# Swapping the halves of the rotated rows by on-chip transfers instead of by permutation matmuls

## The reference, cut to what matters

```python
def apply_partial_rope(x, cos, sin):
    xr = x[..., :ROT_DIM].astype(jnp.float32)            # ROT_DIM = 32
    x1, x2 = xr[..., : ROT_DIM // 2], xr[..., ROT_DIM // 2:]
    rot = jnp.concatenate([x1 * cos - x2 * sin, x2 * cos + x1 * sin], axis=-1)
    return jnp.concatenate([rot.astype(x.dtype), x[..., ROT_DIM:]], axis=-1)
...
    k, v = jnp.split(rms_norm(x, kv_norm) @ w_kv, 2, axis=-1)
    k = apply_partial_rope(k.reshape(bsz, seq, N_HEADS, HEAD_DIM), cos, sin)
...
    q = apply_partial_rope((h @ w_q).reshape(bsz, seq, N_HEADS, HEAD_DIM), cos, sin)
```

## Time and profile before

| | us |
|---|---|
| median of three runs | 1744.65 (1742.34 to 1746.13) |
| the profiled execution, its own time | 1747.92 |
| its span | 1746.2 |
| PE busy in the span | 1541.4 (88%) |
| DVE busy | 872.5 (50%) |
| ACT busy | 658.7 (38%) |
| key rotation, first PE matmul to last DVE sum | 448.07 to 457.35 |
| query rotation, first PE matmul to last DVE sum | 499.38 to 508.76 |

### The profile page before, as it was taken

One profiled execution on the slowest core, in us unless ns is written; L12 is line 12 of the kernel. 1 busy time (PEld: TensorE's weight loads), 2 busy tenths in 40 slices (PEclk: granted clock), 3 DMA queues, 4 the chain that ended last, 5 costly groups with the idle time before them and its releaser, 6 DMA issues.

```text
span 1746.2 us, 34026 instructions
## 1 busy us (share of the span) xinstructions
PE 1541.4 (88%) x14278; PEld 1321.5 (76%) x14278; DVE 872.5 (50%) x1259; ACT 658.7 (38%) x869; POOL 149.6 (9%) x188
## 2 busy tenths in 40 slices
PE   9999999999999999999999999899998565665558
PEld 8999899988988989997898899688975232332334
DVE  5865456645656546665576689876641010101011
ACT  5545354435445435543456745535441000000001
POOL 5900000000000000000006001130110000000000
PEclk9999999999999999999999999899999777787789
DMA  8765656774743766664455244102899999999995
GB/s 250 254 204 172 192 155 184 216 265 154 252 149 118 269 193 188 187 193 165 134 165 174 73 150 151 40 27 74 303 399 413 430 430 429 430 431 432 430 431 248
DMA packets 238129, 417.09 MB, mean 239 GB/s; under 512 B 13698, under 2 KB 213929, under 8 KB 228009
## 3 DMA queue, kind: packets, MB, share of 16 engines
q1 hardware_dynamic: 237817, 414.59, 66.0%
q10 hardware_dynamic: 176, 0.53, 0.1%
HBM read 414.04 MB, written 1.05 MB: 238 GB/s over the span
## 4 chain that ended last, share of the span: by engine, by line
issue 47%; PE 41%; DVE 4%; POOL 4%; ACT 3%; DMA 1%; DVEq 0%; POOLq 0%; SPq 0%; ACTq 0%
PE bank L429 5%; PE bank L430 4%; PE bank L431 4%; PE bank L445 2%; PE bank L447 2%; PE bank L446 2%; PE bank L1922 2%; PE bank L1075 1%; PE bank L1077 1%; PE bank L1076 1%; PE bank L761 1%; POOL ang L912 1%; POOL ang L913 1%; PE bank L457 1%; PE bank L458 1%
## 5 line engine op out<-in xcount | busy, mean ns | idle before, releaser
L250 DVE TENSOR_TENSOR w_lo<-w_raw,w_hi 128x2048 fp32r<-128x2048 f32 (+2 forms) x178 | 402.9, 2267 | 246.3 <-ACT w_hi L243 246.2
L243 ACT ACTIVATE w_hi<-w_raw 128x2048 fp32r<-128x2048 f32 (+2 forms) x178 | 333.8, 1879 | 155.3 <-DMA w_raw<-in_ffn_w_down_dram 58.9
L429 PE MATMUL bank<-h_hi,w_hi 128*128 128x256 f32 x1168 | 328.0, 281 | 6.6 <-DVE h_lo L639 3.8
L431 PE MATMUL bank<-h_hi,w_lo 128*128 128x256 f32 x1168 | 326.9, 280 | 0.0
L430 PE MATMUL bank<-h_lo,w_hi 128*128 128x256 f32 x1168 | 326.9, 280 | 0.0
L429 PEld LDWEIGHTS bank<-h_hi,w_hi 128*128 128x128 f32 x1168 | 220.8, 189 | 8.1 <-issue 7.8
L431 PEld LDWEIGHTS bank<-h_hi,w_lo 128*128 128x128 f32 x1168 | 221.4, 190 | 0.0
L430 PEld LDWEIGHTS bank<-h_lo,w_hi 128*128 128x128 f32 x1168 | 219.4, 188 | 0.0
L2800 PE MATMUL bank<-w_exp_four,xeT 128*32 128x256 f32 x1600 | 133.6, 503 | 95.0 <-DMA w_exp_four<-in_w_up_dram 57.3
L2800 PEld LDWEIGHTS bank<-w_exp_four,xeT 128*32 128x32 f32 x1600 | 66.0, 143 | 161.7 <-issue 86.0
L2933 ACT ACTIVATE sg<-bank 128x256 f32<-128x256 f32 x16 | 6.1, 383 | 391.5 <-PE bank L2800 391.5
(11 more groups left out here) (536 smaller groups left out, 3101.2 us busy)
## 6 DMA issues: line engine op xcount, KB each, us to landing
w_exp_four<-in_w_up_dram SPq DMA_DIRECT2D x13, 4096.0 KB, 33.5
w_exp_four<-in_w_down_dram SPq DMA_DIRECT2D x13, 4096.0 KB, 33.5
w_exp_four<-in_w_gate_dram SPq DMA_DIRECT2D x12, 4096.0 KB, 33.3
w_raw<-in_ffn_w_gu_dram SPq DMA_DIRECT2D x88, 512.0 KB, 5.0
w_raw<-in_w_in_dram SPq DMA_DIRECT2D x54, 512.0 KB, 4.7
w_mod<-in_w_mod_dram SPq DMA_DIRECT2D x24, 1024.0 KB, 7.4
w_raw<-in_ffn_w_down_dram SPq DMA_DIRECT2D x44, 512.0 KB, 4.2
w_raw<-in_mem_w_kv_dram SPq DMA_DIRECT2D x32, 512.0 KB, 4.5
```

Source lines behind the costliest of these rows:

```text
L243: e.activation(whi[slot][:, 0:w], raw[slot][:, 0:w], ACT.Copy).then_inc(S["hi_ready"], 1)
L250: e.tensor_tensor(wlo[slot][:, 0:w], raw[slot][:, 0:w], whi[slot][:, 0:w].bitcast(F32), ALU.subtract).then_inc(S["lo_ready"], 1)
L429: e.matmul(dst, whi[slot][:, lo:hi_], bh[:, k, :], start=begin, stop=False)
L431: ins = e.matmul(dst, wlo[slot][:, lo:hi_], bh[:, k, :], start=False, stop=end)
```

## The change

The matrix `swap1` and its eight matmuls are gone. The halves change places by DMA: ACT issues two transfers for each half of the heads (four heads, 16 partitions by 4 KB each, 64 KB) from `kT` or `qT` to `xn_rope`, one for features 16 to 31 to partitions 0 to 15, one the other way. The sign stands in the sine table now, which ACT makes with the scale `sign1` (-1 for partitions 0 to 15, 1 for 16 to 31). DVE makes for each half of the heads a product with the sine, one with the cosine, and a sum, six instructions of 32 by 1024 instead of four of 32 by 512 and two of 32 by 2048. Line numbers with 11xx in this section are those of the changed kernel (L1141 the transfers, L1169 the products, L1172 the sum).

```diff
-    swap1 = place("swap1", [ROT, ROT], F32)
+    sign1 = place("sign1", [ROT, 2], F32)
...
+            signed = {"scale": sign1[:, 0:1]} if (j, q) == (0, 1) else {}
+            t_rope = act.do(lambda e, ...: e.activation(
+                tab[:, q, :], angles[0:n_, 2 * j + q, :], ACT.Sin, **signed), t_ang, t_sign)
...
+    def swap_rows(buf, tmp, hf):
+        ks = slice(4 * hf, 4 * hf + 4)
+        def run(e):
+            for to, from_ in ((0, ROT // 2), (ROT // 2, 0)):
+                e.dma_start(tmp[to:to + ROT // 2, ks, :], buf[from_:from_ + ROT // 2, ks, :]).then_inc(rows_swapped[hf], 16)
+        return run
+    def copy_and_swap(buf, tmp, ready):
+        evacs = st.evac_a
+        swap = swap_rows(buf, tmp, 0)
+        def chunk(e, c, u, ch):
+            if c == 2:
+                e.wait_ge(S["act_evac"], evacs + 2)
+                e.wait_ge(*ready)
+                swap(e)
+            return copy_fm(buf)(e, c, u, ch)
+        return chunk
+    def rope_rows(buf, tmp, tab, evacs):
+        swaps["n"] += 1
+        swap = swap_rows(buf, tmp, 1)
+        def last_swap(e):
+            e.wait_ge(*evacs)
+            swap(e)
+        act.raw(last_swap)
+        for hf in range(2):
+            landed = (rows_swapped[hf], 32 * swaps["n"])
+            b3, t3 = (v_[0:ROT, 4 * hf:4 * hf + 4, :] for v_ in (buf, tmp))
+            times = lambda v_, q: dve.do(lambda e: e.tensor_tensor(v_, v_, tab[:, q:q + 1, :].broadcast_to((ROT, 4, SEQ)), ALU.mult),
+                                         landed, t_rope, evacs)
+            ts, tc = times(t3, 1), times(b3, 0)
+            t = dve.do(lambda e, b3=b3, t3=t3: e.tensor_tensor(b3, b3, t3, ALU.add), ts, tc)
+        return t
...
-    gemm(4, cols(A["w_kv"]), ..., act_chunk=copy_fm(kT), ready=[th], act_ready=[th2])
+    gemm(4, cols(A["w_kv"]), ..., act_chunk=copy_and_swap(kT, xn_rope, th2), ready=[th], act_ready=[th2])
-    t1 = rope_fm(kT, KT, rope1, swap1, ROT, [t_k, th2], xn_rope)
+    t1 = rope_rows(kT, xn_rope, rope1, t_k)
-    gemm(4, cols(A["moba_w_q"][0]), ..., act_chunk=copy_fm(qT), ready=[th2], act_ready=[t_memkv],
+    gemm(4, cols(A["moba_w_q"][0]), ..., act_chunk=copy_and_swap(qT, xn_rope, t_memkv), ready=[th2], act_ready=[t_memkv],
-    t1 = rope_fm(qT, KT, rope1, swap1, ROT, [t_q, t_memkv], xn_rope)
+    t1 = rope_rows(qT, xn_rope, rope1, t_q)
```

More of the change, by code:

```diff
@@ L553, in build @@
     pool.do(lambda e: e.memset(ident[:, :], 0.0))
-    t = pool.do(lambda e: e.memset(swap1[:, :], 0.0))
+    t = pool.do(lambda e: e.memset(sign1[:, :], -1.0))
+    t_sign = pool.do(lambda e: e.affine_select(out=sign1[:, :], in_=sign1[:, :], compare_op=ALU.is_ge, fill=1.0,
+                                               base=ROT // 2 - 1, pattern=[[0, 2]], channel_multiplier=-1), t)
     t_id = pool.do(lambda e: e.affine_select(out=ident[:, :], in_=ident[:, :], compare_op=ALU.not_equal,
@@ L564, in half_swap @@
         return t
-    t = half_swap(swap1[:, :], ROT, t_id)
-    t_swap = t
+    t_swap = t_id
     for n_ in range(4):
@@ L972, in build @@
         for q in range(2):
-            t_rope = act.do(lambda e, j=j, q=q, tab=tab, n_=n_: e.activation(tab[:, q, :], angles[0:n_, 2 * j + q, :], ACT.Sin), t_ang)
+            signed = {"scale": sign1[:, 0:1]} if (j, q) == (0, 1) else {}
+            t_rope = act.do(lambda e, j=j, q=q, tab=tab, n_=n_, signed=signed: e.activation(
+                tab[:, q, :], angles[0:n_, 2 * j + q, :], ACT.Sin, **signed), t_ang, t_sign)
     gemm(4, cols(A["conv_w_out"][0]), tm_chunk(a_hi, a_lo), dve_chunk=add_tm(x), ready=[t_conv_out])
@@ L1127, in rope_fm @@
         return dve.do(lambda e: e.tensor_tensor(b3, b3, tmp[0:rows, 0:tiles, :], ALU.add), t)
+    rows_swapped = [nc.alloc_semaphore(f"rows_swapped{hf}") for hf in range(2)]
+    swaps = {"n": 0}
+    def swap_rows(buf, tmp, hf):
[29 more added lines that the diff above has]
+        return t
     mem_attention(0, h2, (h_hi, h_lo), lambda k: kT[:, k, :], 1)
@@ L1138, in build @@
                          behind=tiles_of[th])
-    gemm(4, cols(A["w_kv"]), fm_chunk(h_hi, h_lo), act_chunk=copy_fm(kT), ready=[th], act_ready=[th2])
+    gemm(4, cols(A["w_kv"]), fm_chunk(h_hi, h_lo), act_chunk=copy_and_swap(kT, xn_rope, th2), ready=[th], act_ready=[th2])
     t_k = act_evacs()
@@ L1149, in build @@
     t_memkv = split_features(turn_rows(xn, rows), lambda k: col("norm_memkv", 8 + k), [all_used()])
-    gemm(4, cols(A["moba_w_q"][0]), fm_chunk(*h2), act_chunk=copy_fm(qT), ready=[th2], act_ready=[t_memkv],
+    gemm(4, cols(A["moba_w_q"][0]), fm_chunk(*h2), act_chunk=copy_and_swap(qT, xn_rope, t_memkv), ready=[th2], act_ready=[t_memkv],
          beside={j: mod_load(0, j) for j in range(4)})
```

## The result

The changed kernel takes 1759.51 us (median of 4 runs, 1756.18 to 1762.26), the kernel before 1743.49 (4 runs, 1741.78 to 1746.13). The ratio is 1.0107, with an interval of 1.0079 to 1.0135: **slower by 1.1%, some 16 to 19 us**, where 5 us less had been forecast. The profiled execution took 1761.23 us, with a span of 1759.5; its counterpart before has 1746.2.

A forecast was written before the change was run, and what follows sets the result against it. PE, busy 88% of the span, was taken as the bound; 2.5 us at the keys plus 4.4 at the queries, less 1.5 of clock, gave 5.4 us off the median 1744.65: 1739.3 us, range 1736.2 to 1743.3.

The forecast's parts named there:

- What bounds the kernel: Whole kernel: PE is busy for 88% of the span, no other engine for more than half.
- PE's part of the sum: Permutation and slow matmuls removed on PE: 5.2 us at the keys, 6.9 at the queries, 12.1 if PE alone decided.
- the case with both pauses: Rival: both new PE pauses, at keys and queries, cost lower clock; gain 3.9 us, 1740.8 us; chance 0.37.
- DVE: Rotation on DVE: six instructions of 1.23 us, about 7.2 us together against 7.35 before, so the rotation hardly ends earlier.
- V3: Keys: V3's split stands behind the rotation, so PE waits 2.7 us and 2.5 of 5.2 us are left.
- The softmax and the turning: Queries: PE waits 1.1 us before the scores, 3.0 before turning the probabilities; the softmax starts 4.4 us earlier.
- The transfers: On-chip swaps at keys and queries: 0.46 us of ACT per issue, landing in 3.2 us, delaying nobody.
- spare of 2.2 us: Second half of the heads, keys and queries: its transfers land 2.2 us before DVE is ready for them.
- late landing: Rival: transfers land one to three us late at both places, so the rotation's second half waits; 1742.3 us; chance 0.08.
- weight loads ahead: Rival: transfers stand behind weight loads and take 15.1 us; 12.5 us lost, 1757.2 us; chance 0.03.
- The clock: PE's two new pauses, 2.7 and 3.0 us: one is followed by lower clock, costing 1.5 us.
- the forecast's 5.4: Main case: 6.9 us from both places, less 1.5 us for one pause's lower clock, 1739.3 us; chance 0.42.

The follow-up runs named there:

- experiments 9 and 10: The kernel before (9) and the changed kernel (10), both with the features 64 bytes higher than in the kernel before: 1759.57 us and 1755.51 us.
- experiment 1: The changed kernel with 96 unused bytes behind sign1, so later tensors have their addresses of the kernel before: 1740.69 us, ratio 1.0006.
- Experiment 4: The changed kernel with the 96 bytes put back and V3's split ahead of the memory's normalization: 1736.41 us, ratio 0.9973 to the kernel before.
- experiment 8: The kernel before with 32 bytes ahead of w_raw, moving weights and features together: 1740.40 us, ratio 1.0001.
- experiments 13 and 14: Changed kernel, V3's split first, M3's low part behind the first softmax, features 32 bytes lower (13) or 96 higher (14) than before: 1751.98 and 1742.67 us.
- experiment 12: Changed kernel with the 96 bytes put back, V3's split ahead of the memory's normalization, M3's low part behind the first softmax: 1735.99 us, 0.9967 to the kernel before.
- 7: The changed kernel with the 96 bytes put back behind x, so only x and the rope tables stay moved: 1743.81 us, ratio 1.0020 to the kernel before.
- 6: The changed kernel with the sign columns inside neg_half, features 128 bytes lower than in the kernel before: 1739.92 us, ratio 0.9993 to the kernel before.
- experiment 3: The changed kernel with 32 bytes behind sign1, features 64 bytes lower than in the kernel before: 1751.47 us, ratio 1.0076 to the kernel before.

## Why the prediction was wrong, point by point

- **What bounds the kernel**: right. **PE's part of the sum** (12.1 us): the permutation's 7.8 us went, with the slow stretches behind it. But the slow stretch at the queries, 2.9 us of the sum, is in two of six traces of kernels with the permutation only, and the one at the keys in five. Without the former the two places won 1.7 us in the traces of experiments 9 and 10, where the case with both pauses had 3.9.
- **DVE**: right. 7.24 us for six instructions, forecast 7.2, at 1.21 each (1.23).
- **V3**: the mechanism right. A wait of 3.07 us in the changed kernel, 2.95 in experiment 1, where 2.7 was expected. The profile puts it down to ACT; but the `w_hi` that it names is a later chunk's, and PE started at 472.30, when the low part of V3, the first of these three (2.29 us each), had just ended at 472.2:

```profile
469.91 6.86 DVE L250 TENSOR_TENSOR w_lo<-w_raw,w_hi 128x2048 fp32r<-128x2048 f32 x3 [2.23 <-ACT w_hi L243]
```

  Experiment 4 shows that the order of the queues was at fault.
- **The softmax and the turning**: right. 0.72 and 2.67 us of wait against 1.1 and 3.0; at the scores the profile names ACT's `keys2a`, which ended at 517.91, but DVE's last sum ended at 517.89: the two came together.
- **The transfers**: mis-sized and harmless. The landing is not 3.2 us, and the issue is not 0.46. The tile's rows, issue in ns (min/median/max) and first and last start, with the landing:

```profile
L1141 ACTq DMA_DIRECT2D xn_rope<-kT x4: 514/604/1132, 446.6 to 453.7; - x4
L1141 ACTq DMA_DIRECT2D xn_rope<-qT x4: 514/560/612, 500.0 to 507.0; - x4
DMA to landing us min/median/max: 3.9/4.7/6.1
```

  The spare of 2.2 us over 3.2 covers the median, and DVE shows no idle time before any of its six instructions at the keys. A pair of issues held ACT for up to 1.76 us (446.61, the pair ahead of K2's evacuation) where 0.9 was expected; the split behind was early enough. The late landing and the weight loads ahead (1757.2 us, which by accident is close to the result) did not happen: the slower time has another cause, and the number agreeing would have misled whoever did not look at 418 us.
- **The clock**: the forecast let one pause cost 1.5 us. Both did (the second case, 0.37), in experiment 10 by 1.8 and 1.5 us of its lead. The 4.1 us between the medians of experiments 9 and 10 are near that case's 3.9 and the forecast's 5.4, and too uncertain to choose between them.
- **The step that failed** is a term that the sum (2.5 us at the keys, 4.4 at the queries, less 1.5 of clock) put at nothing without a reason. It counted what the change adds and removes in the queues, and took `sign1` in place of `swap1`, the first lines of the diff, for no cost at all, without naming what lies behind them in memory. This term measured some 18 us (ratio 1.0107 for the change, 1.0006 with the 96 bytes put back; 2.9 ns on 6,500 starts are 19), against 2 to 4 for all the others together, and of the other sign. The range (1736.2 to 1743.3) and the 0.02 for slower had no room for it, as each case in them began at the rotation. A rival "the 96 bytes matter" had no price in any row of before; but the rows that could have warned were there: the pace was two-valued (0.118 for the keys' products, 0.114 behind the queries, both in the prediction's own sums) and I used both without asking why the same instruction has two.

## What to carry to other kernels

Where tensors are placed one behind the other, an edit that resizes a small one moves every later one; keep the addresses (pad, or put the new tensor last) when you test an idea, and time the pad alone as a control. When a change costs or brings more than its place can explain, compare the start of the same instruction in both traces well ahead of the edit, and then the distance of PE's starts, not durations or busy shares. And try a few paddings between stationary and moving operands of a matmul-bound kernel: here two pads alone put the same kernel 19 us apart (ratios 1.0001 in experiment 8, 1.0111 in 9), more than any edit of the order won.

Read a small win against the scatter of single executions, too: a stretch of low clock that stands in one trace (here the 2.9 us behind the query permutation) may be missing in the next.

## What the runs showed of the hardware

- A stream of 128x256 float32 matmuls at full clock starts every 113.3 to 120.0 ns, by the signed distance in SBUF between its two operands (table under experiments 13 and 14). The Trainium skill (TensorE: Matmul & The Clock Gate, "Wait — 56ns, not 53.3ns?") gives N ÷ 2.4 GHz and about 2.5 ns from start to start; for 256 columns that makes an estimate of 109.2 ns. All measured paces here lie above it, and they are not one number.
- At shifts 0 and -128 the pace has two levels, 113.3 and 117.8 ns, and one can hold for long within an execution (201 to 472 us in the kernel before); at +64 there is one, 120.0.
- Waits of PE of 2.4 to 3.9 us were mostly followed by a clock of 0.50, for 3.4 us (2.95 in experiment 1, 2.4 and 2.7 in 10, 3.9 in 7, 2.67 in the change) or 6.8 us (3.07 in the change, 3.6 in 6); one of 2.7 in experiment 1 and two of 2.7 in experiment 3 by none. At 1.6 us none fell in experiment 12; but 1.2 us without matmuls from 970.6 us on were followed there by 3.4 us at 0.50.
- Eight 32x32x512 matmuls, in which PE was shown busy for 3.6 to 4.0 us, were followed by a clock of 0.50 in seven of twelve places (six traces), for 3.4 or 6.8 us.
- An on-chip transfer of 64 KB, issued by ACT while weights were loading, landed after 3.9 to 6.1 us and held ACT's queue for 0.51 to 1.13 us.
